# A two-block network kernel on one core: six re-orderings around waits, from the first modulation sums to the last tiles

## The reference, cut to what matters

```python
mod = jax.nn.silu(c) @ w_ada[l] + b_ada[l]          # first block: shift, scale, gate columns
h = rms_norm(x, norm1_g[l]) * (1.0 + scale1) + shift1
...
def cross_attention(h, mem, wq, wkv, wo):           # second block, 4 heads of 256, 256 memory rows
    q = (h @ wq); k, v = jnp.split(mem @ wkv, 2, axis=-1)
    s = einsum("bshd,bmhd->bhsm", q, k) / sqrt(256)
    p = softmax(s, axis=-1)
    return einsum("bhsm,bmhd->bshd", p, v).reshape(B, S, 1024) @ wo
def swiglu(h, w_in, w_out):                         # D_FF = 2816
    a, b = jnp.split(h @ w_in, 2, axis=-1)
    return (silu(a) * b) @ w_out
x = x + hybrid_mixer(rms_norm(x, norm_mix_g), ...)  # ends with @ w_out ("wo2")
x = x + cross_attention(rms_norm(x, norm_x_g), mem, ...)
x = x + swiglu(rms_norm(x, norm_ffn_g), ...)
return rms_norm(x, final_norm_g)
```

## Time and profile before

| | |
|---|---|
| three runs | 2127.91, 2125.6, 2128.12 us; median 2127.91 |
| the profiled execution | 2126.63 us, of which the span 2124.7 us |
| mean granted TensorE clock | 0.962 of full speed |
| busy: PE, DVE, ACT, POOL | 1944.8, 751.6, 604.2, 662.3 us |
| moved by DMA | 361.96 MB |

### The profile page before, as it was taken

How to read it: one execution, slowest core, us unless ns; L and a number is a source line. 1 busy time by engine, 2 the same in 40 slices (tenths; PEclk the granted TensorE clock), 3 DMA queues, 4 the chain that set the end, 5 groups by cost and what they waited for, 6 DMA issues and landing times.

```text
span 2124.7 us, 22145 instructions
## 1 busy us (share of the span) xinstructions
PE 1944.8 (92%) x8760; PEld 1264.1 (59%) x8760; DVE 751.6 (35%) x1522; ACT 604.2 (28%) x1082; POOL 662.3 (31%) x384
## 2 busy tenths in 40 slices
PE   4999989599889899989999999988899889999997
PEld 3544337433333333368889868644588578888886
DVE  6551265612222222254898024366321220000002
ACT  3113462111000011062232243466333432222211
POOL 0011333311110111054442224555344224555532
PEclk8999899799999999999997998999999999999999
DMA  9452001879999999942322321110132122232221
GB/s 382 158 223 89 0 1 65 320 293 427 428 426 428 428 426 429 398 170 80 119 79 80 100 79 50 60 31 21 60 139 79 40 89 80 80 119 80 108 91 60
DMA packets 89477, 361.96 MB, mean 170 GB/s; under 512 B 5883, under 2 KB 34939, under 8 KB 74796
## 3 DMA queue, kind: packets, MB, share of 16 engines
q1 hardware_dynamic: 86672, 351.75, 42.5%
q0 software_dynamic: 2304, 8.39, 1.0%
q10 hardware_dynamic: 412, 0.59, 0.1%
HBM read 355.41 MB, written 5.31 MB: 170 GB/s over the span
## 4 chain that ended last, share of the span: by engine, by line
PE 72%; DMA 13%; DVE 6%; ACT 5%; issue 2%; POOL 1%; SPq 0%; DVEq 0%; ACTq 0%
PE bank L730 14%; PE bank L731 14%; PE bank L732 14%; PE bank L705 11%; DMA slots<-in_w_expert_gate 9%; PE bank L1068 7%; DMA slots<-in_w_expert_up 3%; PE bank L1298 2%; PE bank L1278 2%; PE bank L858 1%; PE bank L1093 1%; ACT area L1812 1%; POOL low_r L2559 1%; PE bank L1039 1%; DMA slots<-in_w_ada 1%
## 5 line engine op out<-in xcount | busy, mean ns | idle before, releaser
L2559 POOL TENSOR_TENSOR low_r<-slots,high_r 128x2048 fp32r<-128x2048 f32 x87 | 401.3, 4614 | 603.5 <-ACT high_r L1483 603.5
L731 PE MATMUL bank<-xl_r,high_r 128*128 128x512 f32 (+1 forms) x864 | 330.3, 382 | 0.0
L730 PE MATMUL bank<-area_r,high_r 128*128 128x512 f32 x800 | 313.8, 392 | 1.1 <-POOL low_r L2559 1.1
L732 PE MATMUL bank<-area_r,low_r 128*128 128x512 f32 x800 | 312.2, 390 | 0.0
L1483 ACT ACTIVATE high_r<-slots 128x2048 fp32r<-128x2048 f32 x87 | 166.3, 1914 | 430.0 <-PE bank L732 418.5
L1068 PE MATMUL bank<-slots,area 128*64 128x512 f32 x992 | 230.3, 609 | 26.5 <-DMA slots<-in_w_expert_gate 19.4
L731 PEld LDWEIGHTS bank<-xl_r,high_r 128*128 128x128 f32 x864 | 163.1, 189 | 31.6 <-issue 0.5
L1068 PEld LDWEIGHTS bank<-slots,area 128*64 128x64 f32 x992 | 68.3, 139 | 172.3 <-issue 128.7
L730 PEld LDWEIGHTS bank<-area_r,high_r 128*128 128x128 f32 x800 | 151.0, 189 | 33.1 <-POOL low_r L2559 1.3
L732 PEld LDWEIGHTS bank<-area_r,low_r 128*128 128x128 f32 x800 | 150.7, 188 | 31.4
L2387 DVE SCALAR_TENSOR_TENSOR bank<-area,cols,bank 128x512 f32<-128x512 f32 x232 | 153.5, 753 | 0.0
(11 more groups left out here) (390 smaller groups left out, 2886.8 us busy)
## 6 DMA issues: line engine op xcount, KB each, us to landing
slots<-in_w_expert_up SPq DMA_DIRECT2D x32, 2048.0 KB, 16.4
slots<-in_w_expert_down SPq DMA_DIRECT2D x32, 2048.0 KB, 17.2
slots<-in_w_expert_gate SPq DMA_DIRECT2D x30, 2048.0 KB, 15.2
slots<-in_w_in SPq DMA_DIRECT2D x15, 2048.0 KB, 8.4
slots<-in_w_ada SPq DMA_DIRECT2D x11, 2048.0 KB, 12.2
slots<-in_ffn_in_w SPq DMA_DIRECT2D x22, 1024.0 KB, 7.2
slots<-in_ffn_out_w SPq DMA_DIRECT2D x5, 2048.0 KB, 7.8
slots<-in_w_out SPq DMA_DIRECT2D x4, 2048.0 KB, 7.9
```

The source lines that it names most:

```text
L730: nc.tensor.matmul(out, xh, yh, start=start and n == 0, stop=False)
L731: nc.tensor.matmul(out, xh, yl, start=False, stop=False)
L732: last = nc.tensor.matmul(out, xl, yh, start=False, stop=stop and n == len(pairs) - 1)
L2559: nc.gpsimd.tensor_tensor(low_half(m), raw_half(m), high_half(m), ALU.subtract).then_inc(s["w_low"], 1)
```

## The change

In PE's list `ada_columns(1)` goes ahead of the first norm's transposes. In ACT's `norm`, `ahead_of_root` goes ahead of the wait for the last tile. "wo2" starts when four low parts of `GCS` are there, and waits for the rest at its second half. The first two cross-attention scores are made between the two halves of the second "xq" chunk, with their exponentials ahead of ACT's fifth query bank; the score banks change their order to 4, 5, 2, 3; POOL makes the second low half of "xo" after steps 0 and 1. The feed-forward norm is made tile by tile inside the residual, with a root made early on a dummy column. For "ffout", f 0 to 17 run as before and the last four f run inside the loop over tiles and column halves; the last half of the weights has its high part in a third place (`xl_r`); the final norm is made per tile and per column half, the gain ahead of the inverse root, half of the last scaling on ACT. The sums of squares go to new places, and `var_ready` and `std_ready` count four for each norm.

```diff
@@ high_half, and the last high part's wait in ACT's split_weights
+            if m == len(HALVES) - 1:
+                return xl_r[:, 2048:4096]
             return high_r[:, m % 2 * 2048:m % 2 * 2048 + HALVES[m][2]]
...
-                    if m >= 2:
+                    if m == len(HALVES) - 1:
+                        act.wait_ge(s["proj_done"], FIRST["ffin"] + 2 * FT)
+                    elif m >= 2:
                         act.wait_ge(s[HALVES[m - 2][3]], HALVES[m - 2][4])
@@ PE, start
             ada_columns(0)
+            ada_columns(1)
             norm_transposes("norm1", XN1)
-            for j in range(1, 4):
+            for j in range(2, 4):
                 ada_columns(j)
@@ PE, wo2
-            pe.wait_ge(s["tile_low"], 3 * KT)
+            pe.wait_ge(s["nsa_kept"], NH // 2)
+            pe.wait_ge(s["tile_low"], 2 * KT + 4)
             for n in range(2):
-                split_token_major("wo2", GCS, C, n)
+                split_token_major("wo2", GCS, C, n, more_tiles=3 * KT)
@@ PE, cross attention (split_groups calls `between` after half 0)
+            def first_scores():
+                pe.wait_ge(s["act_emptied"], emptied("act", FIRST["xq"] + 1))
+                x_scores(0)
+                x_scores(1)
+
+            split_feature_major("xq", hTS, 0, later_columns="normx")
             split_emptied("normx")
+            split_feature_major("xq", hTS, 1, between=first_scores)
+            all_emptied(FIRST["xq"] + 8)
             pe.wait_ge(s["xv_loaded"], 16)
-            x_scores(0)
-            x_scores(1)
@@ PE, ffout
+            for f in range(FT - 4):
                 if f % 2 == 0:
-                    wh, wl = parts(FIRST_HALF["ffout"] + f // 2, 2)
+                    w = parts(FIRST_HALF["ffout"] + f // 2, 2)
                     pe.wait_ge(s["tile_low"], 3 * KT + f + 2)
                 for t in range(TT):
                     for half in range(2):
+                        last = ffn_out(f, t, half, w)
+                if f % 2 == 1:
                     last.then_inc(s["ff_used"], 1)
+            w = [parts(len(HALVES) - 2, 2), parts(len(HALVES) - 1, 2)]
+            pe.wait_ge(s["tile_low"], 3 * KT + FT)
+            for t in range(TT):
+                for half in range(2):
+                    for f in range(FT - 4, FT):
+                        last = ffn_out(f, t, half, w[(f - FT + 4) // 2])
+                    last.then_inc(s["ff_full"], 1)
@@ ACT, norm by tile and norm
+            def norm_by_tile(XN, ready, first):
+                def root(t):
+                    act.wait_ge(s["var_ready"], TT * k + t + 1)
+                    nc.scalar.activation(std4[:, t:t + 1], var4[:, t:t + 1], ACT.Sqrt).then_inc(s["std_ready"], 1)
+                for t in range(TT):
+                    act.wait_ge(ready, first + t)
+                    nc.scalar.activation(XN[:, t, :], X[:, t, :], ACT.Square, accum_out=ssq[:, t:t + 1]
+                                         ).then_inc(s["ssq_ready"], 1)
+                    if t:
+                        root(t - 1)
+                root(TT - 1)
...
                 for t in range(TT):
+                    if t == TT - 1 and ahead_of_root is not None:
+                        ahead_of_root()
                     if ready is not None:
                         act.wait_ge(ready, first + t)
-                    if t == TT - 1 and ahead_of_root is not None:
-                        ahead_of_root()
@@ ACT, cross attention and the norm after it
             for c in range(KT):
                 if c % 4 == 0:
                     split_weights(FIRST_HALF["xq"] + c // 2 + 3)
+                if c == 4:
+                    x_exponent(0)
+                    x_exponent(1)
...
-            norm(XN4, s["dve_emptied"], emptied("dve", FIRST["xo"] + 4))
+            nc.scalar.activation(small[:, 153:154], small[:, 152:153], ACT.Sqrt)
+            norm_by_tile(XN4, s["dve_emptied"], emptied("dve", FIRST["xo"] + 4))
@@ ACT, the end
-            norm(A(0, 4096, TT), s["x_ff"], 1)
+            for t in range(TT):
+                for half in range(2):
+                    act.wait_ge(s["x_ff"], 2 * t + half + 1)
+                    nc.scalar.activation(SQO[2 * t + half], X[:, t, half * C:(half + 1) * C], ACT.Square,
+                                         accum_out=half_ssq[:, 2 * t + half:2 * t + half + 1]
+                                         ).then_inc(s["ssq_ready"], 1)
...
+                nc.scalar.activation(last_std[:, t:t + 1], half_ssq[:, 2 * t + 1:2 * t + 2], ACT.Sqrt,
+                                     bias=last_bias[:, t:t + 1], scale=1.0 / D).then_inc(s["std_ready"], 1)
+                act.wait_ge(s["rstd_ready"], t + 1)
+                nc.scalar.activation(XO[:, t, 0:C], XO[:, t, 0:C], ACT.Copy, scale=last_rstd[:, t:t + 1]
+                                     ).then_inc(s["x_final"], 1)
@@ DVE, residual with XN given (tile_variance: variance; tile_scaled: reciprocal and scaling)
+                    if half and XN is not None:
+                        if t:
+                            tile_variance(t - 1)
+                        if t == TT - 1:
+                            tile_variance(t)
+                        if t:
+                            tile_scaled(XN, t - 1)
+                        if t == TT - 1:
+                            tile_scaled(XN, t)
@@ DVE, the end, for each half
+                    nc.vector.tensor_tensor(X[:, t, piece], banks[2 * t + half][:, :], X[:, t, piece], ALU.add
+                                            ).then_inc(s["x_ff"], 1)
+                    nc.vector.tensor_tensor(XO[:, t, piece], X[:, t, piece], FG2[:, piece], ALU.mult
+                                            ).then_inc(s["x_gained"], 1)
...
+                nc.vector.reciprocal(last_rstd[:, t:t + 1], last_std[:, t:t + 1]).then_inc(s["rstd_ready"], 1)
+                nc.vector.tensor_scalar(XO[:, t, C:2 * C], XO[:, t, C:2 * C], last_rstd[:, t:t + 1], None, ALU.mult
+                                        ).then_inc(s["x_final"], 1)
@@ POOL
-            low_weights(FIRST_HALF["xo"] + 2)
+            low_weights(FIRST_HALF["xo"] + 1)
             for w in range(16):
+                if w == 2:
+                    low_weights(FIRST_HALF["xo"] + 2)
```

More of the change, by code:

```diff
@@ L417, in build @@
         FG2 = A(4096, D)
+        XO = A(0, 4096, TT)
+        SQO = [A(19696 + i * C, C) for i in range(4)] + [slot(3)[:, i * C:(i + 1) * C] for i in range(4)]
+        half_ssq, last_bias, last_std, last_rstd = (small[:, 224:232], small[:, 232:236], small[:, 236:240],
+                                                    small[:, 240:244])
         g_dram = dram("bias_falling", [NH, NG])
@@ L679, in _ @@
             for t in range(TT):
-                sp.wait_ge(s["x_final"], TT + t + 1)
-                sp.dma_start(io["out"][0, t * P:(t + 1) * P, :], X[:, t, :]).then_inc(s["out_done"], 16)
+                sp.wait_ge(s["x_final"], TT + 2 * t + 2)
+                sp.dma_start(io["out"][0, t * P:(t + 1) * P, :], XO[:, t, :]).then_inc(s["out_done"], 16)
             sp.wait_ge(s["out_done"], 16 * TT)
@@ L738, in parts, with split_groups @@
                 return (high_half(m).rearrange("p (k n) -> p k n", k=k), low_half(m).rearrange("p (k n) -> p k n", k=k))
-            def split_groups(stage, n, tiles, width, operands, more_tiles=0, later_columns=None):
+            def split_groups(stage, n, tiles, width, operands, more_tiles=0, later_columns=None, between=None):
                 for half in range(2):
@@ L757, in split_groups @@
                         last.then_inc(s["half_used"], 1)
+                        if between is not None:
+                            between()
             def split_token_major(stage, x, n_cols, n=0, tiles=TT, more_tiles=0):
@@ L1395, in _, with ffn_out @@
             split_emptied("ffn")
-            for f in range(FT):
+            def ffn_out(f, t, half, w):
+                tokens, out_cols = slice(t * P, (t + 1) * P), slice(half * C, (half + 1) * C)
+                return split_product(banks[2 * t + half][:, :],
+                                     [(GTH[f][:, tokens], GTL[:, f, tokens], w[0][:, f % 2, out_cols],
+                                       w[1][:, f % 2, out_cols])], start=f == 0, stop=f == FT - 1)
+            for f in range(FT - 4):
                 if f % 2 == 0:
-                    wh, wl = parts(FIRST_HALF["ffout"] + f // 2, 2)
+                    w = parts(FIRST_HALF["ffout"] + f // 2, 2)
                     pe.wait_ge(s["tile_low"], 3 * KT + f + 2)
@@ L1835, in _, with x_exponent @@
             split_columns("normx", cols[:, V_XN:V_XN + KT])
+            def x_exponent(w):
+                act.wait_ge(s["x_scored"], w + 1)
+                if w >= 4:
+                    act.wait_ge(s["x_t_full"], w - 3)
+                nc.scalar.activation(PX[:, w % 4, :], banks[(4, 5, 2, 3)[w % 4]][:, 0:MEM], ACT.Exp,
```

(18 more changed lines are left out.)

61 lines of the change are left out of this document (33 added, 28 removed).

## The result

The changed kernel takes 2103.18 us (median of four runs, 2100.43 to 2105.52) against 2126.76 for the kernel before on the same chip: a ratio of 0.989, 95% interval 0.9875 to 0.9905. That is 23.6 us or 1.1% faster. The direction was forecast, but 2111.7 and its range down to 2107.5 were too slow. The profiled execution took 2103.7, its span 2101.9.

A forecast was written before the change was run, and what follows sets the result against it. It took TensorE (PE) to bound the kernel, busy 92% of the span. Six terms summed to 16.2 us, taking the profiled execution from 2126.63 to 2110.4 and the median to 2111.7, range 2107.5 to 2117.

The forecast's parts named there:

- first sums: Kernel start: DVE's fourth sum follows the third without its wait, so the first projection starts sooner; 3.95 us, bounds 2.5 to 5.5.
- value weights: Value weights: ACT's fourth high part moves earlier and PE's gap before the fourth half closes; 2.0 us, bounds 0.8 to 2.1.
- wo2: Second output projection: PE starts 1.98 us sooner and the low clock afterwards may vanish; 2.6 us, bounds 1.9 to 3.7.
- cross attention: Cross attention: two steps' transposes go early, then a 3.4 us stop at step 2; 0.7 us, bounds 0.2 to 2.1.
- feed-forward norm: Before the feed-forward transposes: early root table and scaling by tile let PE start sooner; 1.65 us, bounds 0.7 to 2.4.
- last tiles: Last product and final norm: shorter end behind PE's last matmul, less a 0.6 us stop; 5.3 us, bounds 3.7 to 6.2.
- I expect each to pass through: Whole kernel: later triggers hang on PE's progress, so every term's gain reaches the end; 16.2 us in sum.
- Rival (b): Changed stages: the clock favours the change, terms mostly at their upper bounds; gain 21.0, so 2106.9 us; chance 0.09.
- (g): Table loads: by the page, two hidden loads are worth 2.8 us more than counted; 2109 us; chance 0.02.
- (d): Last weight chunk lands late, at 8 us, and PE waits 3.7 us, not 0.6; 2114.8 us; chance 0.05.
- (a): Clock goes against the change, low after each shortened stop; gain 12.6, so 2115.3 us; chance 0.14.
- (c): Experts' stage: its stream of loads absorbs the first sums' gain; 2115.7 us; chance 0.06.

The follow-up runs named there:

- the lone parts: Runs of the kernel before with one part of the diff each, plus the new places for the sums of squares and new counts; ratios 0.9975 to 0.9996.
- the first profile: Profiled execution of the changed kernel in its first measurement, against the kernel before; it took 2103.7 us, the median of those runs 2103.18.
- only_value_weights: Kernel before with the value weights' part alone (ACT's `ahead_of_root` ahead of the wait for the last tile): 2121.14 us, ratio 0.9975.
- the third profile: Profile of the changed kernel when run a third time with no edit: 2104.55 us, ratio 0.9897 to the kernel before.
- the second: Profile of the changed kernel when run again with no edit: 2107.78 us, ratio 0.9906 to the kernel before.
- The lone part: Kernel before with the first sums' part alone (`ada_columns(1)` ahead of the first norm's transposes): 2122.82 us, ratio 0.9988.
- only_cross: Kernel before with the early cross-attention scores alone, POOL's second low half of "xo" after steps 0 and 1: 2125.71 us, ratio 0.9996.

## Why the prediction was too small

The changed kernel's 14 runs have a median of 2105.0 (2099.4 to 2108.3), the 79 runs of before 2126.1: 21 us. So of the miss of 8.5 us, some 2 are the chance of the first four runs. All 14 lie below 2111.7.

| term | predicted | measured (from the table and the lone parts) |
|---|---|---|
| first sums | 3.95 | 2.3 to 3.2 at the experts' end; 3.9 alone |
| value weights | 2.0 | 2.1 |
| wo2 | 2.6 | 3.6 |
| cross attention | 0.7 | -0.8 |
| feed-forward norm | 1.65 | 2.8 |
| last tiles | 5.3 | 5.2 |
| sum | 16.2 | 15.8 (with 2.9 for the first) |
| untouched stretches | 0 | 3.5 in each profile, and 3.1 more in one of three |

**The step that failed** is the one behind the sum: "I expect each to pass through", with the clock weighed only where an edit stands. The terms' sum was right within 0.4, but by luck: wo2 and the feed-forward norm were 1.0 and 1.15 too low, the first sums 1.0 and cross attention 1.5 too high. What was missing is 1.8 between 1160 and 1254, 1.5 at the first outputs of "xo" (eight matmuls of L705 in 5.23 us before, of L711 in 3.70 after; the rest of the table's 4.3 is the norm's 2.8), about 0.2 between 1254 and 1504, and in the first profile 3.1 ahead of "wo2". All but the 0.2 are stretches at the low level that end sooner or stay away. Only the 1.8 is tied to an edit by a lone run (only_value_weights), and not firmly; the 1.5 and the 3.1 are against a fall that versions with the same work up to there also lack, so they may be luck of the profiles compared. Why these falls come or go stays open. Rival (b), the clock in favour, at 0.09, came nearest, yet mostly for a reason that it did not have: it placed its gains in the changed stages, and there only "wo2" and the feed-forward norm got them.

**First sums.** The wait went as forecast, and the first projection starts 4.3 to 5.1 sooner, above the 3.95 and within 2.5 to 5.5. Between 73 and 450 us 1.3 to 2.9 are given back. In the first and the third profile the low level in the first attention lasts from 199 to 226 instead of 206 to 226; in the second that stretch is as long as before. What arrives at the experts' end, 2.3 to 3.2, is under the low bound of 2.5 in one profile of three. The lone part kept 3.9. I leave open what decides between them.

**Value weights.** Right, in the first of the two orders that it named: 2.1 in the stage. What followed 220 us later (1.8) was not in it.

**wo2.** 1.98 of the wait, 2.00 measured. The fall that followed (0.57) is gone in all seven profiles with the short stop and there in all eight with the long one; I took 0.6 for it, it was 1.6, so 3.6 in all, within the bounds.

**Cross attention.** The mechanism was exact: two transposes, then a stop of "3.4 us", measured 3.54. The low level around it was under-priced: the clock is at 0.57 in the window from 1642 to 1650, a fall of 6.8 us in all three profiles and in only_cross, of which PE works through 5.4 to 5.7, against a fall of 3.4 before. The total fell under the bound of 0.2, to a loss of 0.8.

**Feed-forward norm.** The tiles couple less than I had it: I made the last add 0.72 late, it was 0.29 late (1723.33, where 1714.88 and three tiles of 2.72 would give 1723.04). From the last square to the last scaling it takes 0.2 less than I had, so the stop is 4.24 and not 4.9. The transposes run 0.5 us faster behind it, which I had not counted. (g) is refuted: the load alone gave 0.94.

**Last tiles.** All parts right: a stop of 0.6 (0.63), a transfer that lands in 4.9 us again, which refutes (d) (its 8 us were those of 2 MB loads outside the experts; this one has 1 MB), and 5.9 us from PE's last matmul to the end against "about 6". (a), (c), (e) and (f) did not happen as a whole; of (a), cross attention fell below its low bound, and the low level in the first attention was longer in two profiles.

## What to carry to other kernels

When a wait is moved to the next consumer and returns there at its old length, look at what stands ahead of that consumer in the releasing engine's list: here a 4.5 us subtraction, due only at the second half of "xo", 11 us after "xo" begins, cost 6 us because it stood ahead of a step's scaling of half a microsecond, for which PE waited. Price a stop of PE as the stop plus the low level that goes with it; shortening "wo2"'s stop by 2.0 gave 3.6. A sum of waits can be right and the time still miss by the falls elsewhere, so compare several executions place by place before a few microseconds are put down to an edit.

## What was unexpected of the hardware

- The granted clock of one kernel differs between executions. Single stretches at the low level come and go: near 1292 (worth 6.3 us, absent in 3 of 15 profiles), ahead of "wo2" (3.1 us, absent in 3 of 15). Runs of before spread over 9 us (2119.5 to 2128.4), and a lone part of 3 us has an interval of 4.
- In the experts' stage there are none to five falls in a profile, 61 us apart where there are several, at no cost that the profiles show (454.5 us with two, 454.7 with five, 455.3 with none).
- Removing the stop in the value weights went with a shorter low stretch 220 us later in five of seven profiles, and a longer one in two. Why a stop so far ahead should matter is not settled by these runs.
- An early table load is worth 0.94 us where its row says 1.28, since it had run beside another engine's work.
